# A gated recurrence and sparse attention layer on one core: the recurrence's share of the output projection moved ahead of the attention, and the rank scans given a zero from PSUM

## What is computed

```
    z = h @ w_in[l]
    xr, gr, q, k, v, ga, qi, ki, wi = jnp.split(z, split_points, axis=-1)
    y_r = rg_lru(causal_depthwise_conv(xr, ...), ...) * jax.nn.silu(gr)
    y_a = dsa_attention(...) * jax.nn.silu(ga)
    y = jnp.concatenate([y_r, y_a], axis=-1) @ w_out[l]
    x = x + gate[:, None, :] * y
return rmsnorm(x, final_g)
```

## Time and profile before

| | us |
|---|---|
| median of 3 runs (620.45 to 621.84) | 620.57 |
| the profiled execution | 619.93 |
| its span, first to last instruction | 618.1 |
| PE busy | 535.4 (87%) |
| PE loading weights, beside its products | 444.8 (72%) |
| DVE busy | 439.5 (71%) |
| ACT busy | 377.4 (61%) |
| POOL busy | 233.5 (38%) |

### The profile page before, as it was taken

One profiled execution on the slowest core, in us unless ns is written; L12 is line 12 of the kernel. 1 busy time (PEld: TensorE's weight loads), 2 busy tenths in 40 slices (PEclk: granted clock), 3 DMA queues, 4 the chain that ended last, 5 costly groups with the idle time before them and its releaser, 6 DMA issues.

```text
span 618.1 us, 8029 instructions
## 1 busy us (share of the span) xinstructions
PE 535.4 (87%) x2676; PEld 444.8 (72%) x2676; DVE 439.5 (71%) x992; ACT 377.4 (61%) x679; POOL 233.5 (38%) x195
## 2 busy tenths in 40 slices
PE   1459989998999999999999526489999999999994
PEld 1346868777787777778888415478889999888873
DVE  5987386885999889898697886854475666664522
ACT  6513236453499999987898555554466666656531
POOL 5150862352344274677642003740402030313322
PEclk9859999998999999999999855569999999999999
DMA  8967342430112111135550420110011000101011
GB/s 335 418 206 266 105 118 53 102 85 18 36 34 69 34 36 34 35 103 137 140 133 0 177 96 0 68 36 2 8 61 43 28 36 34 41 30 69 0 69 68
DMA packets 16457, 51.96 MB, mean 84 GB/s; under 512 B 4000, under 2 KB 5024, under 8 KB 15392
## 3 DMA queue, kind: packets, MB, share of 16 engines
q1 hardware_dynamic: 16416, 51.45, 26.3%
HBM read 37.81 MB, written 4.19 MB: 68 GB/s over the span
## 4 chain that ended last, share of the span: by engine, by line
PE 68%; DVE 11%; DMA 7%; POOL 5%; ACT 4%; issue 3%; SPq 2%; DVEq 0%; POOLq 0%; ACTq 0%
PE pair L1373 30%; PE pair L1470 13%; PE pair L1492 6%; PE pair L1505 5%; DMA ada<-in_ada_w 4%; PE pair L1448 3%; PE pair L1449 2%; DMA qs<-half_lo 2%; PE pair L1422 2%; DVE rank L1156 2%; PE pair L1514 2%; PE pair L1413 2%; PE pair L1414 2%; DVE tie L1158 1%; POOL half_lo L726 1%
## 5 line engine op out<-in xcount | busy, mean ns | idle before, releaser
L1373 PE MATMUL pair<-h_hi,w_hi 128*128 128x512 f32 (+1 forms) x352 | 114.4, 407 | 1.6 <-DVE h_lo L1064 1.5
L1373 PE MATMUL pair<-h_lo,w_hi 128*128 128x512 f32 (+1 forms) x352 | 109.8, 393 | 0.0
L1373 PE MATMUL pair<-h_hi,w_lo 128*128 128x512 f32 (+1 forms) x352 | 109.0, 391 | 0.0
L1298 DVE TENSOR_TENSOR pt_lo<-pair,pt_hi 128x512 fp32r<-128x512 f32 (+3 forms) x96 | 50.5, 554 | 71.1 <-ACT pt_hi L963 70.5
L858 ACT ACTIVATE bias_sb<-score_sb,tinies 128x1024 bf16<-128x1024 f32 (+2 forms) x93 | 95.7, 1032 | 3.2 <-DVE tinies L1109 3.1
L696 POOL TENSOR_SCALAR w_hi<-w_raw 128x1024 fp32r<-128x1024 f32 (+1 forms) x22 | 29.4, 1339 | 136.3 <-PE pair L1373 120.5
L1373 PEld LDWEIGHTS pair<-h_hi,w_hi 128*128 128x128 f32 (+1 forms) x352 | 65.0, 188 | 19.0 <-issue 6.2
L1373 PEld LDWEIGHTS pair<-h_lo,w_hi 128*128 128x128 f32 (+1 forms) x352 | 66.0, 188 | 15.5 <-issue 0.8
L1373 PEld LDWEIGHTS pair<-h_hi,w_lo 128*128 128x128 f32 (+1 forms) x352 | 65.6, 186 | 15.4 <-issue 0.7
L1095 DVE TENSOR_SCALAR_CACHE_REDUCE bias_sb<-score_sb,tinies 128x640 bf16<-128x640 f32 (+2 forms) x93 | 72.6, 802 | 0.9
L781 POOL TENSOR_TENSOR x_res<-q_free,x_res 128x512 f32<-128x512 f32 x14 | 18.1, 1296 | 121.0 <-DVE q_free L1269 121.0
(11 more groups left out here) (195 smaller groups left out, 1254.2 us busy)
## 6 DMA issues: line engine op xcount, KB each, us to landing
w_raw<-in_w_tiles SPq DMA_DIRECT2D x21, 512.0 KB, 3.5
ada<-in_ada_w SPq DMA_DIRECT2D x8, 1024.0 KB, 18.4
x_sb<-in_x SPq DMA_DIRECT2D x8, 512.0 KB, 7.1
ada_g<-in_ada_w SPq DMA_DIRECT2D x8, 512.0 KB, 4.5
qs<-half_hi SPq DMA_DIRECT2D x16, 256.0 KB, 3.6
qs<-half_lo SPq DMA_DIRECT2D x16, 256.0 KB, 4.4
wo_raw<-in_w_out SPq DMA_DIRECT2D x8, 512.0 KB, 6.4
x_res<-in_x SPq DMA_DIRECT2D x8, 512.0 KB, 3.3
```

Source lines behind the costliest of these rows:

```text
L1298: nc.vector.tensor_tensor(pt_lo[:, 4 * b:4 * b + nc4, hh, :], psum[use % 2][:, 0:nc4 * P].rearrange("p (c q) -> p c q", q=P), f32(pt_hi[:, ...
L1373: ins = nc.tensor.matmul(psum[banks[half]][0:width, :], w[b][:, k, 0:width], hh[:, k, half * HALF:(half + 1) * HALF], start=(k == 0 and p ...
```

## The change

1. The recurrence's half of the output projection (blocks 0 to 3 of `w_out`) is taken out of the pieces and made as 16 *parts*, one for each half of a tile, 12 matmuls each (`part_of`). Parts 0 to 3 stand ahead of the attention in PE's order; parts 4 to 15 in its steps 0 to 11, behind the scores. ACT copies each from PSUM to SBUF (`part_evac`): parts 0 to 2 ahead of its loop, the others at the head of steps 0 to 12. SP writes them into `out` in device memory and reads them back tile by tile (`part_load`); POOL multiplies by the gate and adds them to the residual (`base_of`), ahead of the first tile and then behind each tile's last gain.
2. The pieces are now four a tile, of the attention's blocks alone, in steps 8 ti + 14, 16, 18 and 20; in steps 70 to 73 for the last tile.
3. POOL makes both halves of blocks 0 to 3 of `w_out`, ACT the high half of blocks 4 to 7 alone, in steps 2 to 5. The first two `yr_hi` are events of the planner, when their buffers (in the place of the last weight slabs) come free; the others follow behind the odd parts' copies.
4. The rank scan has a zero column in PSUM, spread over its length, as second input, and the limit's arithmetic is halved to fit.

The diff, cut to its core:

```diff
-WO_START = 5
-OUT_START = 20
-PIECES = {g: [2 * (g - OUT_START), 2 * (g - OUT_START) + 1] for g in range(OUT_START, 2 * OUT_START - LAG_OUT)}
-PIECES.update({g: [g - LAG_OUT] for g in range(2 * OUT_START - LAG_OUT, LAST_STEP)})
+FIRST_PARTS = 4
+PARTS = 2 * NT
+WO_POOL = CT
+WO_START = 2
+PIECES = {8 * ti + LAG_OUT + 1 + (2 * p if ti < NT - 1 else p): [4 * ti + p] for ti in range(NT) for p in range(4)}
...
+    for b in range(2):
+        add("ACT", ("yrh", b), 0.7, 1, ("kstep", NJ - 2 + b, KC - 1), ("yr", CT - 1))
...
+        yr_hi = [sb(f"yr_hi{b}", R_W + 18432 + 2048 * b, [P, CT, P], F32R) for b in range(2)]
+        part = [sb(f"part{b}", R_W + 12288 + 2048 * b, [P, HALF]) for b in range(2)]
...
+        part_in = [sb(f"part_in{b}", R_YR + 4096 * b, [P, D]) for b in range(2)]
...
+        zero_ps = psum[7][:, HALF - 1:HALF]
...
+        def part_bank(e):
+            return 2 if e < FIRST_PARTS and e % 2 else 3
...
+            for e in range(PARTS):
+                ti, half = divmod(e, 2)
+                i = ATT[ti]
+                sp.wait_ge(part_ev, e + 1)
+                sp.dma_start(out[i * P:(i + 1) * P, half * HALF:(half + 1) * HALF], part[half][:, :]).then_inc(part_out[half], 16)
+            def part_load(ti):
+                i = ATT[ti]
+                for half in range(2):
+                    sp.wait_ge(part_out[half], 16 * (ti + 1))
+                sp.dma_start(part_in[ti % 2][:, :], out[i * P:(i + 1) * P, :]).then_inc(part_back[ti % 2], 16)
             sp.wait_ge(bias_ok, len(PICK))
             sp.wait_ge(halves_ok, len(RAW_USE))
             sp.wait_ge(evac_done, len(EVAC))
+            sp.wait_ge(part_ps, PARTS)
             for ti in range(2):
                 sp.dma_start(x_res[ti][:, :], x[ATT[ti] * P:(ATT[ti] + 1) * P, :]).then_inc(xres_in[ti], 16)
+                part_load(ti)
...
+                    sp.wait_ge(base_ok, ti + 1)
+                    part_load(ti + 2)
...
-            for m in range(KC):
-                pool.wait_ge(wo_hi_ok, m + 1)
-                nc.gpsimd.tensor_tensor(wo_lo[:, m, :], wo_raw[:, m, :], f32(wo_hi[:, m, :]), ALU.subtract).then_inc(wo_ok, 1)
...
+            def split_wo(m):
+                if m < WO_POOL:
+                    pool.wait_ge(wo_in[m], 16)
+                    nc.gpsimd.tensor_scalar(wo_hi[:, m, :], wo_raw[:, m, :], 1.0, 0.0, ALU.mult, ALU.add).then_inc(wo_hi_ok, 1)
+                pool.wait_ge(wo_hi_ok, m + 1)
+                nc.gpsimd.tensor_tensor(wo_lo[:, m, :], wo_raw[:, m, :], f32(wo_hi[:, m, :]), ALU.subtract).then_inc(wo_ok, 1)
             split_yr(0)
-            split_yr(1)
+            for m in range(WO_POOL):
+                split_wo(m)
+            for ti in range(1, 4):
+                split_yr(ti)
+            for ti in range(4, NT):
+                split_wo(ti)
+                split_yr(ti)
+            def base_of(ti):
+                b = ti % 2
+                pool.wait_ge(part_back[b], 16 * (ti // 2 + 1))
+                nc.gpsimd.tensor_tensor(part_in[b][:, :], part_in[b][:, :], gate_bc[:, :], ALU.mult).then_inc(part_mul, 1)
+                pool.wait_ge(xres_in[b], 16 * (ti // 2 + 1))
+                pool.wait_ge(part_mul, ti + 1)
+                nc.gpsimd.tensor_tensor(x_res[b][:, :], x_res[b][:, :], part_in[b][:, :], ALU.add).then_inc(base_ok, 1)
+            base_of(0)
...
-                    pool.wait_ge(xres_in[ti % 2], 16 * (ti // 2 + 1))
+                    pool.wait_ge(base_ok, ti + 1)
...
-                if ti + 2 < NT:
-                    split_yr(ti + 2)
...
+                    base_of(ti + 1)
...
+                if o[0] == "yrh":
+                    act.wait_ge(proj_done, NJ - 1 + o[1])
+                    act.wait_ge(rnn_done, CT)
+                    yr_half(o[1])
...
+            def part_evac(e):
+                ti, half = divmod(e, 2)
+                act.wait_ge(part_ps, e + 1)
+                if ti:
+                    act.wait_ge(part_out[half], 16 * ti)
+                nc.scalar.activation(part[half][:, :], bank(part_bank(e)), ACT.Copy).then_inc(part_ev, 1)
+                if half and ti + 2 < NT:
+                    yr_half(ti + 2)
+            for e in range(FIRST_PARTS - 1):
+                part_evac(e)
             for g in range(LAST_STEP + 1):
-                if g == OUT_START - 4:
+                if 0 <= g + FIRST_PARTS - 1 < PARTS:
+                    part_evac(g + FIRST_PARTS - 1)
...
+                if WO_START <= g < WO_START + KC - WO_POOL:
+                    m = WO_POOL + g - WO_START
...
+                link(nc.vector.memset(zero_ps, 0.0))
...
-                link(nc.vector.tensor_tensor_scan(rank[i][:, :], tie[i][:, :], tie[i][:, :], float(2 * n - 4 * TOPK), ALU.add, ALU.add))
-                link(nc.vector.tensor_scalar(cols(c, nK), rank[i][:, n - 1:n], 0.5, cols(c, cnt), ALU.mult, ALU.subtract))
+                link(nc.vector.tensor_tensor_scan(rank[i][:, :], tie[i][:, :], zero_ps.to_broadcast([P, n]), float(n - 2 * TOPK), ALU.add, ALU.add))
+                link(nc.vector.tensor_scalar(cols(c, nK), rank[i][:, n - 1:n], cols(c, cnt), 0.5, ALU.subtract, ALU.mult))
...
-                            dve.wait_ge(xres_in[ti % 2], 16 * (ti // 2 + 1))
+                            dve.wait_ge(base_ok, NT)
...
+            def part_of(e):
+                ti, half = divmod(e, 2)
+                i = ATT[ti]
+                if e < 2:
+                    pe.wait_ge(evac_done, len(EVAC) - 1)
+                elif e <= FIRST_PARTS:
+                    pe.wait_ge(part_ev, e - 1)
+                else:
+                    pe.wait_ge(part_ev, e)
+                if half == 0:
+                    pe.wait_ge(yr_ok, ti + 1)
+                for m in range(CT):
+                    if e == 0:
+                        pe.wait_ge(wo_ok, m + 1)
+                    y2 = (yr_hi[ti % 2][:, m, :], yr_lo[:, m, i * P:(i + 1) * P])
+                    for p, (y, w) in enumerate(((y2[0], wo_hi), (y2[0], wo_lo), (y2[1], wo_hi))):
+                        ins = nc.tensor.matmul(bank(part_bank(e)), y, w[:, m, half * HALF:(half + 1) * HALF],
+                                               start=(m == 0 and p == 0), stop=(m == CT - 1 and p == 2))
+                ins.then_inc(part_ps, 1)
+            for e in range(FIRST_PARTS):
+                part_of(e)
...
+                if g + FIRST_PARTS < PARTS:
+                    part_of(g + FIRST_PARTS)
                 for o in PIECES.get(g, ()):
-                    ti, piece = divmod(o, 8)
-                    i = ATT[ti]
-                    half = piece // 4
-                    if piece % 4 == 0:
-                        if 2 * ti + half:
+                    ti, piece = divmod(o, 4)
+                    half = piece // 2
+                    if piece % 2 == 0:
+                        if o == 0:
+                            pe.wait_ge(part_ev, PARTS)
+                            pe.wait_ge(wo_ok, KC)
+                        else:
                             pe.wait_ge(y_ok, 2 * ti + half)
-                    if ti == 0 and piece < 4:
-                        pe.wait_ge(wo_ok, 2 * piece + 2)
                     if piece == 0:
-                        pe.wait_ge(yr_ok, ti + 1)
-                    if piece == 2:
                         pe.wait_ge(ya_ok, ti + 1)
-                    for m in (2 * (piece % 4), 2 * (piece % 4) + 1):
-                        if m < CT:
-                            y2 = (yr_hi[ti % 2][:, m, :], yr_lo[:, m, i * P:(i + 1) * P])
-                        else:
-                            y2 = (ya_hi[ti % 2][:, m - CT, :], ya_lo[ti % 2][:, m - CT, :])
+                    for m in (CT + 2 * (piece % 2), CT + 2 * (piece % 2) + 1):
+                        y2 = (ya_hi[ti % 2][:, m - CT, :], ya_lo[ti % 2][:, m - CT, :])
```

51 lines of the change are left out of this document (29 added, 22 removed).

## The result

The changed kernel takes 649.04 us (median of 4 runs, 647.8 to 651.26) beside 620.51 for the kernel before in the same runs: a ratio of 1.046, 95% interval 1.043 to 1.050. It is **28.5 us slower**, where 644 was forecast. Its profiled execution took 651.26, its span is 649.5, 31.4 more than before.

The account below looks back on a forecast made before the run. PE leads, but the prediction expected moved work to leave rings of engines waiting for each other. 618.1 + 41 to the mark - 18.8 late - 0.5 tail + 2 for the clock gave span 641.8; forecast 644 us, range 616 to 665.

Parts of the forecast that it names:

- the mark: Start of the PV product of pair 7 (step 17), end of the early stage; forecast at 450.9, 41 us late.
- the tail: Stretch from pair 31's PV product to the end; forecast 26.2 us instead of 26.7.
- The start: Early stage: parts 0 to 3, waiting for split w_out, put head 0's scores at 380.0, 33 us later.
- without this cover: Early stage: masks of columns 3 to 5, hidden by the wait for parts 0 to 3, would otherwise cost 8 us.
- The ring of the parts: Steps 0 to 11: part, transposes, pt_hi, exponential, evacuation, next part never overlap; 4.6 us a step, 5.3 with PV.
- case (c): Rival, early stage: PE's clock is at half for all twelve parts, 26 us more, 670; chance 0.1.
- The late stage: Pairs between those of 7 and 31: 24.8 us gained, less 3 for transposes and 3 for scaling, net 19 us earlier.
- three steps of room: Middle of the kernel: POOL's two added operations per tile, 4.8 us, have three steps of room.
- the pair's term: Late stage: a pair with 1024 keys takes 8.1 us instead of 8.73, 0.63 gained; with 640 keys 3.2 gained.
- (a): Rival: PE alone is the bound in both stages; 608 us, faster; chance 0.13.
- (b): Rival: only the late stage gains at full price, 644 - 19 = 625 us; chance 0.12.
- (d): Rival, early stage: masks are not covered and POOL's splits make them longer; 14 us more, 658; chance 0.1.

Follow-up runs that it names:

- h2: h1 with ScalarE making early high halves, GpSimd's splits after the masks of columns 3 to 5, parts in steps 4 to 13, later final_g wait; 619.5 us.
- h3: h2 without GpSimd's wait for the masks of columns 3 to 5, so its splits run beside them; 623.7 us.
- e4: The changed kernel with GpSimd's gating and adding of the written half cut to 8 of 1024 columns; 642.7 us.
- h4: h2 with three moved tiles instead of five, six parts at the end of steps 4, 5, 6, 8, 9 and 10; 613.07 us.
- e2: The changed kernel with two matmuls instead of six in each of the 32 late pieces; 649.0 us.
- e7: The changed kernel with the late pieces of the first seven tiles on odd steps instead of even ones; 649.3 us.
- e3: The kernel before with the recurrence's half of the output projection left out, the other pieces at the changed kernel's steps; 602.8 us.
- h1: The changed kernel with only five tiles moved, head 0's scores first, parts at the end of steps 2 to 11; 624.5 us.
- h5: The kernel before, nothing moved, with PSUM scans, full pieces one per step from step 13 and a later final_g wait; 619.45 us.

## Why the prediction came out as it did

Its sum was +41 to the mark, 2 for the clock, -18.8 behind the mark, -0.5 in the tail: +23.7. Measured in the spans: +43.0, -12.4, +0.8: +31.4. The early part is right to the microsecond, by luck: two misses of 3 us cancel. Of the 7.7 us that are left, 6.4 lie behind the mark and 1.3 in the tail.

- **The start.** First scores at 377.4, forecast 380: GpSimd lost nothing to DVE (its blocks follow each other by 3.44 us), where 3 us were added for it; DVE lost to GpSimd instead. The 8 us of masks "without this cover" were about right: 9.0 from h2 to h3. That `yr_hi` on ACT costs 0.6 us during the search was wrong (some 4), but it is covered as well.
- **The ring of the parts.** Forecast 4.6 us for a step without PV and 5.3 with, and 54.1 with the clock's 2 from part 5 to 15. Measured 4.4 to 4.7 and 5.0 to 5.2 in the steps with neither a `wo_hi` copy nor a fall of the clock, 56.8 in all (381.25 to 438.03). The difference is the clock: one fall was allowed for, there were three, 5 us. The stretch of the earlier trace rows, by which I held that the clock stays up, had PE busy for half of 2 us; between the parts it is busy for a third of 3. So case (c) was too large, but its mechanism was there; the rule of the Trainium skill that I set aside ("TensorE: Matmul & The Clock Gate", section "A second HAM failure mode: psum-queue depth-cycling") fits the row of part 7 at 0.64 better than my reading did.
- **The late stage.** Forecast 18.8, measured 12.4. The step that failed is the one that costs the gated sum in the middle at nothing, as it has "three steps of room", and has SP waiting for "nothing else that is due". The first tile has no such room: its sum starts when its parts are read back, at 449.8, and `final_g` is on its way until 454.8, while their user is ready at 452.1. By the prediction's terms the first five pairs gain 12.0 (4 x 3.2 and 0.6, less two transposes of a tile and one scaling); they gained 5.9, and 11.2 in e4, h2 and h4, where neither this stall nor the fall of the clock behind it occurs. The next 19 gain 7.3 by its terms (19 x 0.6, less four transposes and five scalings) and gained 6.5. So the size of the pair's term held, but by luck. 8.1 was forecast for 1024 keys and 8.2 to 8.3 measured; the sum counts the even step's piece (1.38) in full, and this piece adds nothing (e2, e7): it fills a wait for the exponential that the sum didn't have and that happens to be as long as scores, transposes and piece together.
- **The tail.** Forecast 26.2, 27.7 measured; e4 prices the gated sum there at 5.7, where the prediction had 4.8 (2 x 2.4) and set it off against shorter products.
- **The rivals.** (a), PE as the only bound, is refuted by e2 (0 of 29 us gained) and by e3 (17.6 of 44). (b) would have needed the same. (d), the masks, stayed covered; h1 and h3 show that the danger was real once the cover was gone.

## What to carry to other kernels

Before work is moved off a stage, shorten it there once without moving it (thin matmuls, as e2): if the time stays, the stage waits on a ring of other engines, and the busy share of the engine says nothing about what moving gives. Work that is moved into idle time must fit three things: its inputs must be ready when the idle time begins, its order in the step must leave the other engines' chain free (behind the transposes, not before), and its amount must be what the idle time holds; here two or three tiles of eight and not all, if moving pays at all, which h5 leaves open. And when a stage starts late, look for what the delay hides: the 10 us that GpSimd's splits and one early copy cost the masks came out only when the wait in front was taken away.
